# A depthwise convolution on TensorE: eight feature tiles in 32x32 tiles of the array instead of five in full ones

## What is computed

```python
def conformer_conv(h, pw1_w, pw1_b, dw_w, dw_b, ln_g, ln_b, pw2_w, pw2_b):
    u = h @ pw1_w + pw1_b
    u = u[..., :CONV_CH] * jax.nn.sigmoid(u[..., CONV_CH:])
    u = lax.conv_general_dilated(u, dw_w[:, None, :].astype(u.dtype), window_strides=(1,),
                                 padding=[(CONV_WIDTH // 2, CONV_WIDTH // 2)],
                                 feature_group_count=CONV_CH) + dw_b          # 31 taps, one filter per feature
    mu, var = mean and variance of u over the 2048 features
    un = (u - mu) * lax.rsqrt(var + NORM_EPS) * ln_g + ln_b
    return jax.nn.silu(un) @ pw2_w + pw2_b
```

## Time and profile before

| | us |
|---|---|
| median of 3 runs (lowest, highest) | 3243.42 (3241.31, 3244.7) |
| span of the profiled execution | 3244.1 |
| TensorE busy, share of the span | 3021.5, 93% |
| VectorE busy | 2202.5, 68% |
| ScalarE busy | 1244.9, 38% |

### The profile page before, as it was taken

One profiled execution on the slowest core, in us unless ns is written; L12 is line 12 of the kernel. 1 busy time (PEld: TensorE's weight loads), 2 busy tenths in 40 slices (PEclk: granted clock), 3 DMA queues, 4 the chain that ended last, 5 costly groups with the idle time before them and its releaser, 6 DMA issues.

```text
span 3244.1 us, 49985 instructions
## 1 busy us (share of the span) xinstructions
PE 3021.5 (93%) x20896; PEld 2496.8 (77%) x20896; DVE 2202.5 (68%) x2736; ACT 1244.9 (38%) x1430; POOL 217.1 (7%) x394
## 2 busy tenths in 40 slices
PE   5899999778889888999999999999889999999999
PEld 2588987536677766788888888799867888888887
DVE  3677766477887885577777878759974555555554
ACT  1322221174444443344443434343643343434342
POOL 1000000001000000012122121100000000000000
PEclk9799999899999998999999999999989999999999
DMA  9976887790000033668888888756205455555553
GB/s 326 352 273 238 317 289 246 271 368 24 12 14 13 22 67 106 208 230 285 279 295 281 293 292 277 260 166 184 92 23 181 159 194 186 191 185 192 194 182 130
DMA packets 306013, 640.59 MB, mean 197 GB/s; under 512 B 19035, under 2 KB 23937, under 8 KB 303585
## 3 DMA queue, kind: packets, MB, share of 16 engines
q1 hardware_dynamic: 269280, 529.94, 48.3%
q0 software_dynamic: 28384, 94.76, 9.0%
q10 hardware_dynamic: 8128, 12.72, 1.1%
HBM read 623.81 MB, written 13.40 MB: 196 GB/s over the span
## 4 chain that ended last, share of the span: by engine, by line
PE 83%; DVE 9%; DMA 4%; issue 2%; ACT 2%; ACTq 0%; SPq 0%; POOLq 0%; DVEq 0%
PE ps L445 46%; PE ps L463 15%; PE ps L465 7%; DMA raw<-in_ada_w_dram 3%; PE ps L2385 2%; PE ps L1662 2%; DVE rw_scl L1336 1%; DVE rw_mb L1353 1%; PE ps L382 1%; PE ps L1820 1%; PE ps L1772 1%; DVE rw_mt L1356 1%; DVE rw_scc L1339 1%; PE ps L1569 1%; DVE line L752 1%
## 5 line engine op out<-in xcount | busy, mean ns | idle before, releaser
L422 DVE TENSOR_TENSOR split_lo<-raw,split_hi 128x2048 fp32r<-128x2048 f32 (+1 forms) x372 | 849.7, 2285 | 496.7 <-ACT split_hi L410 488.8
L410 ACT ACTIVATE split_hi<-raw 128x2048 fp32r<-128x2048 f32 x368 | 702.1, 1911 | 1180.4 <-PE ps L445 840.3
L463 PE MATMUL ps<-xa,split_hi 128*128 128x512 f32 x2048 | 723.4, 398 | 6.4 <-ACT xa L617 6.4
L465 PE MATMUL ps<-xa,split_lo 128*128 128x256 f32 x2048 | 574.0, 280 | 0.0
L463 PEld LDWEIGHTS ps<-xa,split_hi 128*128 128x128 f32 x2048 | 384.6, 188 | 103.0 <-ACT xa L617 7.4
L445 PE MATMUL ps<-split_hi,hT_hi 128*128 128x512 f32 x1024 | 399.6, 390 | 0.0
L445 PE MATMUL ps<-split_hi,hT_lo 128*128 128x512 f32 x1024 | 398.5, 389 | 0.0
L445 PE MATMUL ps<-split_lo,hT_hi 128*128 128x512 f32 x1024 | 398.4, 389 | 0.0
L465 PEld LDWEIGHTS ps<-xa,split_lo 128*128 128x128 f32 x2048 | 386.5, 189 | 0.2
L445 PEld LDWEIGHTS ps<-split_hi,hT_hi 128*128 128x128 f32 x1024 | 192.2, 188 | 41.4 <-issue 1.8
L445 PEld LDWEIGHTS ps<-split_hi,hT_lo 128*128 128x128 f32 x1024 | 192.2, 188 | 40.2
(11 more groups left out here) (386 smaller groups left out, 4521.1 us busy)
## 6 DMA issues: line engine op xcount, KB each, us to landing
raw<-in_mlp_w_dram SPq DMA_DIRECT2D x256, 1024.0 KB, 5.4
raw<-in_ada_w_dram SPq DMA_DIRECT2D x64, 1024.0 KB, 9.6
raw<-in_mix_in_w_dram SPq DMA_DIRECT2D x48, 1024.0 KB, 5.7
raw<-in_conv_pw_w_dram SPq DMA_DIRECT2D x48, 1024.0 KB, 5.4
gate<-in_ada_w_dram SPq DMA_DIRECT2D x172, 256.0 KB, 5.0
line<-in_ada_w_dram POOLq DMA_DIRECT2D x171, 256.0 KB, 5.1
late<-in_ada_w_dram POOLq DMA_DIRECT2D x85, 256.0 KB, 5.0
tmpa<-in_ada_w_dram SPq DMA_DIRECT2D x84, 256.0 KB, 4.9
```

The lines of the kernel that those rows point to most:

```text
L410: nc.scalar.activation(split_hi[:, c, :, 0:n], raw[:, c, :, 0:n], ACT.Copy).then_inc(hi_done, 1)
L422: nc.vector.tensor_tensor(split_lo[:, c, :, 0:n], raw[:, c, :, 0:n], split_hi[:, c, :, 0:n], ALU.subtract).then_inc(lo_done, 1)
L463: pe.matmul(ps[:, base + j, :], split_hi[:, c, kk, j * P:(j + 1) * P], both, start=(k == 0), stop=False, skip_group_check=True)
L465: mm = pe.matmul(ps[:, base + j, 0:SEQ], split_lo[:, c, kk, j * P:(j + 1) * P], xa_hi[:, k, :], start=False, stop=(k == KT - 1), skip_grou ...
```

## The change

TensorE takes eight feature tiles (8 to 15) instead of five, VectorE eight instead of eleven. A tile is no longer multiplied by 128x128 diagonals: ScalarE writes 32x32 diagonals of a tap's weights for each block of 32 features (`tap_weights`, 128x32 per tap, made from `sel`, the identity repeated four times), and the array is used as 16 tiles of 32 rows by 32 columns. The features of row group r go through column group c with tap 4i + (c - r) mod 4, so in each of eight groups i the four column groups hold four different taps; the row groups write into four PSUM banks. One feature tile leaves 4 x 4 partial results (a bank per row group, a quarter of the partitions per column group). ScalarE copies them to `quarters`, four matmuls with `sel` as stationary operand (`quarters_summed`) add the four column groups of each row group, and ScalarE copies the sum with the bias to `cu` (`tap_output`).

The diagonals of six tiles (`PE_EARLY`) are written during the first pointwise product, behind its splits, into memory that is free then: two in `cu`, two in `gate`, two in `line`. Those of the last two are written between the copies of the tap stage. As `gate` and `line` hold diagonals, GpSimd's loads into them wait for the sixth tile (`tap_ps`).

The column sums for the mean and the variance use `ones[:, 0:32]`, four feature tiles in four column groups at once; the four partial sums are copied by ScalarE, scaled by 1/32, and one full matmul with ones adds them over the partitions and spreads them. Some semaphores are joined under new names (`turned_ps`, `ysp_hi`, `ysp_lo`), with the same order of events.

```diff
-PE_F = 5
-DIAG_SLOTS = 6
+PE_F = 8
+PE_EARLY = 6
+TAP_GROUPS = (TAPS + 3) // 4
...
                 if n == 20:
                     pool.wait_ge(mrow_st, 16 * (ADA_M + ADA_L))
+                    pool.wait_ge(tap_ps, PE_EARLY)
...
+            def tap_weights(f, taps):
+                for t in taps:
+                    ins = nc.scalar.activation(wtap[f][:, t, :], sel[:, :], ACT.Copy, scale=dwc[:, KT - PE_F + f, t:t + 1])
...
             for n in range(8):
                 m, b = M_PW1 + n, n // 2
-                act_split(act, m + 1, m + 1 + B_OFF)
+                act_split(act, m + 1, m + 1 + B_OFF, NB,
+                          (lambda c, f=n - 1: tap_weights(f, range(8 * c, min(8 * c + 8, TAPS)))) if 1 <= n <= PE_EARLY else None)
...
-            act.wait_ge(pe_chunk, 4 * (M_PW1 + 8))
-            for t in range(TAPS):
-                if t >= DIAG_SLOTS:
-                    act.wait_ge(diag_used, t - DIAG_SLOTS + 1)
-                for j in range(PE_F):
-                    ins = nc.scalar.activation(diag[:, t % DIAG_SLOTS, j, :], ident[:, :], ACT.Copy, scale=dwc[:, KT - PE_F + j, t:t + 1])
-                ins.then_inc(diag_a, 1)
+            def tap_quarters(f):
+                act.wait_ge(tap_ps, f + 1)
+                b = 4 * (f % 2)
+                nc.scalar.activation(quarters[:, f % 2, :, :], ps[:, b:b + 4, 0:SEQ], ACT.Copy).then_inc(tap_ev, 1)
+            def tap_output(f):
+                act.wait_ge(tap_ps, f + 2)
+                nc.scalar.activation(cu[:, KT - PE_F + f, :], ps[:, sum_bank(f), SEQ:2 * SEQ], ACT.Identity,
+                                     bias=col_of("dwb", KT - PE_F + f)).then_inc(tap_out, 1)
+            late_taps = [(f, t) for f in range(PE_EARLY, PE_F) for t in range(TAPS)]
+            for f in range(PE_F):
+                tap_quarters(f)
+                for g, t in late_taps[11 * f:11 * f + 11]:
+                    tap_weights(g, [t])
+                if f:
+                    tap_output(f - 1)
+            tap_output(PE_F - 1)
+            act.wait_ge(ln_ps, MEAN_PART)
+            nc.scalar.activation(tmpa[:, 1, 0:SEQ], ps[:, 3, 0:SEQ], ACT.Copy, scale=1.0 / 32).then_inc(ln_ev, 1)
...
-            dve.wait_ge(diag_used, TAPS)
-            for j in range(PE_F):
-                f = KT - PE_F + j
-                steps.inc(V.tensor_scalar(cu[:, f, :], ps[:, j // 2, (j % 2) * SEQ:(j % 2 + 1) * SEQ], col_of("dwb", f), None, ALU.add))
-            convolved()
...
+            def tapped(f):
+                pe.wait_ge(tap_w, f + 1)
+                pe.wait_ge(glu_ok, (KT - PE_F + f) // 4 + 1)
+                if f == 1:
+                    pe.wait_ge(act_ps, 8)
+                elif f >= 2:
+                    pe.wait_ge(tap_ev, f - 1)
+                if f >= 3:
+                    pe.wait_ge(tap_out, f - 2)
+                for i in range(TAP_GROUPS):
+                    for r in range(4):
+                        rows = slice(32 * r, 32 * r + 32)
+                        for c in range(4):
+                            t = 4 * i + (c - r) % 4
+                            if t < TAPS:
+                                mm = pe.matmul(ps[32 * c:32 * c + 32, 4 * (f % 2) + r, 0:SEQ], wtap[f][rows, t, :], gpad[rows, KT - PE_F + f, t:t + SEQ],
+                                               start=(i == 0), stop=(t + 4 >= TAPS), skip_group_check=True)
                 return mm
...
+            def quarters_summed(f):
+                pe.wait_ge(tap_ev, f + 1)
+                if f >= 2:
+                    pe.wait_ge(tap_out, f - 1)
+                for r in range(4):
+                    mm = pe.matmul(ps[32 * r:32 * r + 32, sum_bank(f), SEQ:2 * SEQ], sel[:, :], quarters[:, f % 2, r, :], start=True, stop=True,
+                                   skip_group_check=True)
+                return mm
+            def column_sums(bank, src, b, first, last):
+                for g in range(4):
+                    mm = pe.matmul(ps[32 * g:32 * g + 32, bank, 0:SEQ], ones[:, 0:32], src(4 * b + g), start=first, stop=last, skip_group_check=True)
+                return mm
+            channels = lambda f: cu[:, f, :]
+            for f in range(PE_F):
+                mm = tapped(f)
+                if f:
+                    mm = quarters_summed(f - 1)
+                mm.then_inc(tap_ps, 1)
+            pe.wait_ge(conv_ok, 1)
+            column_sums(3, channels, 0, True, False)
+            pe.wait_ge(tap_out, 4)
+            column_sums(3, channels, 2, False, False)
+            quarters_summed(PE_F - 1).then_inc(tap_ps, 1)
+            pe.wait_ge(conv_ok, 2)
+            column_sums(3, channels, 1, False, False)
+            pe.wait_ge(tap_out, PE_F)
+            column_sums(3, channels, 3, False, True).then_inc(ln_ps, 1)
+            pe.wait_ge(ln_ev, 1)
+            pe.matmul(ps[:, 6, SEQ:2 * SEQ], ones[:, :], tmpa[:, 1, 0:SEQ], start=True, stop=True, skip_group_check=True).then_inc(ln_ps, 1)
             for b in range(4):
                 pe.wait_ge(csq_ok, b + 1)
-                for f in range(4 * b, 4 * b + 4):
-                    mm = pe.matmul(ps[:, 7, 0:SEQ], ones[:, :], gpad[:, f, 0:SEQ], start=(f == 0), stop=(f == KT - 1))
-            mm.then_inc(var_ps2, 1)
+                mm = column_sums(7, lambda f: gpad[:, f, 0:SEQ], b, b == 0, b == 3)
+            mm.then_inc(ln_ps, 1)
+            pe.wait_ge(ln_ev, 2)
+            pe.matmul(ps[:, 7, SEQ:2 * SEQ], ones[:, :], tmpa[:, 1, SEQ:2 * SEQ], start=True, stop=True, skip_group_check=True).then_inc(ln_ps, 1)
```

More of the change, by code:

```diff
@@ L291, in build_trunk @@
             with ExitStack() as t:
-                diag = sb(t, "diag", [P, DIAG_SLOTS, PE_F, P])
+                wtap_late = sb(t, "wtap_late", [P, PE_F - PE_EARLY, 4 * SEQ])
+                quarters = sb(t, "quarters", [P, 2, 4, SEQ])
             xa = sb(s, "xa", [P, KT, 2, SEQ], F32R)
@@ L304, in build_trunk @@
                 cu = sb(t, "cu", [P, KT, SEQ])
+            flat_of = lambda x: x.rearrange("p f t -> p (f t)")
+            wtap_at = ([flat_of(cu[:, KT - PE_F:KT - PE_F + 4, :]), flat_of(cu[:, KT - 4:KT, :]), gate[:, 0:4 * SEQ], gate[:, 4 * SEQ:8 * SEQ],
+                        line[:, 0:2, :].rearrange("p b n -> p (b n)"), line[:, 2:4, :].rearrange("p b n -> p (b n)")]
+                       + [wtap_late[:, n, :] for n in range(PE_F - PE_EARLY)])
+            wtap = [x[:, 0:TAPS * 32].rearrange("p (t c) -> p t c", c=32) for x in wtap_at]
         rw, at = rwkv_memory(nc)
@@ L333, in build_trunk @@
         init_done, sig_done, s_ready = sem("init_done"), sem("sig_done"), sem("s_ready")
-        pt_ps, pt_ok = sem("pt_ps"), sem("pt_ok")
+        pt_ok = sem("pt_ok")
         xt_ok = sem("xt_ok")
         ADA_ORDER = [0, 4, 1, 5, 2, 6, 3, 7]
-        mt_ps, cols_ok = sem("mt_ps"), sem("cols_ok")
+        turned_ps, cols_ok = sem("turned_ps"), sem("cols_ok")
+        PARAMETERS, MOD_ROWS, LAST_ROWS = 1, 2, 3
         norm_std, norm_xn, tr_ps, tr_ts, tr_hi, tr_lo = (sem(n) for n in ("norm_std", "norm_xn", "tr_ps", "tr_ts", "tr_hi", "tr_lo"))
@@ L1903, in build_trunk @@
         DOWN = [4, 6, 0, 2]
[L1904 to L1907, removed]
+        glu_ok, conv_ok, ln_ps, ln_ev, cen_ok, csq_ok, cstd_ok = (sem(n) for n in (
+            "glu_ok", "conv_ok", "ln_ps", "ln_ev", "cen_ok", "csq_ok", "cstd_ok"))
+        un_ok, sgm_ok, sil_ok = (sem(n) for n in ("un_ok", "sgm_ok", "sil_ok"))
+        YSP = 4
+        tap_w, tap_ps, tap_ev, tap_out = (sem(n) for n in ("tap_w", "tap_ps", "tap_ev", "tap_out"))
+        sum_bank = lambda f: 4 * ((f + 1) % 2)
+        MEAN_PART, MEAN, VAR_PART, VAR = 1, 2, 3, 4
         MROW_LOADS = sum(parts_of(l, c + o) for l, c in ((0, 3), (1, 0)) for o in range(2))
@@ L2014, in pool_rest @@
                 if n == 4:
-                    pool.wait_ge(mt_ps, 1)
+                    pool.wait_ge(turned_ps, MOD_ROWS)
                     for b in range(L_BUF):
@@ L2101, in act_rest @@
                 nc.scalar.activation(gpad[:, 4 * p:4 * p + 4, 0:SEQ], cu[:, 4 * p:4 * p + 4, :], ACT.Square).then_inc(csq_ok, 1)
-            act.wait_ge(var_ps2, 1)
-            nc.scalar.activation(tmpa[:, 0, 0:SEQ], ps[:, 7, 0:SEQ], ACT.Sqrt, scale=1.0 / D, bias=epsc[:, 0:1]).then_inc(cstd_ok, 1)
+            act.wait_ge(ln_ps, VAR_PART)
+            nc.scalar.activation(tmpa[:, 1, SEQ:2 * SEQ], ps[:, 7, 0:SEQ], ACT.Copy, scale=1.0 / 32).then_inc(ln_ev, 1)
+            act.wait_ge(ln_ps, VAR)
+            nc.scalar.activation(tmpa[:, 0, 0:SEQ], ps[:, 7, SEQ:2 * SEQ], ACT.Sqrt, scale=1.0 / D, bias=epsc[:, 0:1]).then_inc(cstd_ok, 1)
             for p in range(5):
@@ L2122, in modulation_columns @@
             def modulation_columns():
-                dve.wait_ge(mt_ps, 1)
+                dve.wait_ge(turned_ps, MOD_ROWS)
                 for m, (l, o) in enumerate(((0, 48), (1, 0))):
@@ L2237, in gate_block @@
                 dve.wait_ge(glu_ok, b + 1)
```

(20 more changed lines are left out.)

19 lines of the change are left out of this document (9 added, 10 removed).

## The result

| | us | ratio to the kernel before |
|---|---|---|
| before, median of 4 runs | 3244.06 | |
| changed, median of 4 runs | 3224.96 | 0.9945, 95% interval 0.9931 to 0.9959 |
| changed, once more (6 runs), beside 3245.63 | 3227.73 | 0.9944, 0.9927 to 0.9961 |

The change gains 0.55%, some 19 us, where 43.6 were forecast. The profiled execution spans 3229.0 us against 3244.1.

The account below looks back on a forecast made before the run. TensorE and VectorE both bound the convolution taps, ending within 4 us of one another; afterwards VectorE would be last. Gains of 42.7 us to the centring and 1.1 in the variance gave 43.8, forecast 3200.5 us, range 3196 to 3230.

Parts of the forecast that it names:

- rival (a): Taps on TensorE: small instructions can't be supplied fast enough, 28.3 ns a record, TensorE ends at 2363.4, time 3222; chance 0.24.
- (c): Taps on TensorE: partial overlap or short supply, 8 to 10 us a tile, 3226 at 8.4; chance 0.08.
- VectorE's share: VectorE's taps: eight tiles instead of eleven, ending at about 2342.3, 37 us earlier.
- ScalarE: Writing the 32-column diagonals: 0.25 us each, hidden behind the pointwise products' splits and level with TensorE in the taps.
- The tail: After VectorE's end: centring near 2345.2, root done 8.8 to 9.2 us after centring began, gaining 1.1 us there.
- TensorE's share: Taps on TensorE: eight feature tiles at 4.3 us each from 2302.2, ending at 2337, before VectorE.
- rival (b): Taps on TensorE: row groups take turns, 13.8 + 0.63 us a feature tile, time 3276; chance 0.08.
- The term of 3.7 + 0.63 = 4.3 us: TensorE's time for one feature tile: 3.7 us of overlapped taps plus 0.63 for summing the quarters.
- the quarter sums' part: After each feature tile's taps on TensorE: one round of 0.43 us plus 0.2 for the change of shape.
- GpSimd's queue: Loads moved past the sixth feature tile: bias rows land at 2342, wanted about 2367, hidden with 20 us to spare.
- The clock: TensorE's granted clock: full in the taps, since no gap precedes them; half in the next stage until 2417.
- The second rival under (a): Taps on TensorE: small tiles at half clock, 6.9 us a tile, ending at 2362, time 3222; within the shared 0.24.

Follow-up runs that it names:

- half_columns: Changed kernel with each small tap matmul over 128 of 256 tokens, same 992 matmuls; 3231.27 us, ratio 0.9953.
- double_columns: Changed kernel with each small tap matmul over 512 columns and half the tap groups, 512 matmuls instead of 992; 3200.78 us, ratio 0.9865.
- gates_last: Changed kernel with GpSimd's two 1 MB gate loads moved behind the last feature tile; 3224.07 us, ratio 0.9933.

## Why the prediction was wrong

The median of 3224.96 lies in the stated range (3196 to 3230), near the time of rival (a), 3222. The forecast itself, 3200.5, gained more than twice what came. Rival (a) has the mechanism, but part of its closeness is luck: a feature tile took 8.5 us on average, not its 7.65, and (c), with 8 to 10 us a tile and "supply well under the rate of rows 10" at 0.08, fits the stage better. Its sum is off by 2 us as written: a gain of 15.5 at 8.4 us a tile gives 3228 and not 3226.

**VectorE's share: right.** Its last tap ended at 2342.7 and the small copy behind it at 2342.9, forecast 2342.3.

**ScalarE: right.** Eleven diagonals of 32 columns took 2.43 us, 0.22 each, forecast 0.25; TensorE was never late in the pointwise products (45.00 of 45 us).

**The tail: right.** From the centring to the end of the root 9.1 us, forecast 8.8 to 9.2; to the next product 22.2 instead of 23.1.

**TensorE's share: here it failed.** The step was "I take 3.7, near the lower end, because both directions overlap". They do overlap, all sixteen tiles; rival (b), row groups in turn, is refuted by the starts 17 ns apart. But the rounds are 0.65 us apart and not 0.43, as a round begins only when the first tile's last record has ended. That makes 5.2 us. And the instructions of a feature tile take 7 us to arrive. The term of 3.7 + 0.63 = 4.3 us measured 7.2 in the middle of the stage and (67.8 / 8) 8.5 on average; the quarter sums' part of it, 0.57 at full clock, was priced well. Had I put the double rate of rows 10 beside the rate needed as a bound rather than as a rival with 0.24, the sum would have gone by it: half_columns and double_columns show that it was the binding term. Rival (a) had the mechanism, but its price, 28 ns a record from the densest stretch, was a demand and not a limit: with 2048 records of taps and quarter sums in 67.8 us it came to 33 ns, 7.0 us / 256 = 27 ns undisturbed. That 28 lies so near 27 is luck, as far as the record shows.

**GpSimd's queue: the second miss.** "Hidden with 20 us to spare; were the taps late, both shift together" looked only at who waits for the loads. Who shares the way with them was not asked. The 2 MB met the fetching of TensorE's instructions and cost gaps of 3.47 and 2.25 us, and what followed them at a granted clock of 0.50 (2356.4 to 2370.0), some 7 us in all by gates_last. The same holds, at 2 us, for SyncE's last load. Before the change neither mattered, since three blocks served the whole tap stage.

**The clock: half right.** The second rival under (a) was half clock throughout; it came for 3.4 us twice near the start, and for the last 14 us behind the gaps; with gaps of at most 1.28 us in the same place (gates_last) the clock stayed at full. It also costs more than (a) priced: six rounds took 6.63 us there, 1.10 each, not 0.86.

```profile
2356.40:2370.00 13.60, 11.35 (x289) 6.50 (x284) 0.00 (x0) 1.39 (x2) 1.45 (x4) 0.50 0.36 73
```

## What to carry to other kernels

Cutting a matmul into small tiles multiplies its instructions: count their bytes (here some 256 for each matmul of 32-bit floats) and set the rate beside the highest that a trace has shown the instruction queue to hold over several blocks, before counting columns. Where that supply is the limit, a large transfer in the stretch is in its way, even one that nobody waits for, so large loads go before or behind it. And when two engines share a job, recompute the split with the measured price of a share: here seven tiles beat eight.

## What the runs showed of the hardware

- TensorE's instructions come in blocks of 16 KB through one queue (q8), in no profile here closer than 3.27 us and in the undisturbed taps mostly 3.4 to 3.7 apart, although a block itself is under way for 0.9 to 1.5 us; why it is 3.5 no run here shows. 256 instructions in 3.5 us is 14 ns each, 54 to 55 ns for a matmul of 32-bit floats. In the changed kernel GpSimd's gate loads beside it (200 to 460 GB/s) stretched the distance to 6.0 and 8.0 us, and SyncE's load (some 400 GB/s) to 6.0.
- A TensorE that waits for nothing the profile knows can be waiting for its instructions: 67 gaps over 0.6 us in eight profiles each ended 1.2 to 1.6 us after a block had landed.
- Sixteen 32x32 tiles do compute at the same time. In a stream they start one every 17 ns, and a round of 256 columns starts 0.65 us after the last, one of 512 columns 1.08.
- The speed of the array no longer matters when the instructions are late: with half the columns and a mean granted clock of 0.70 the stage was 65 us, against 67.8 with all columns at 0.85.
